# Sums of squares from squares split into a rounded high part and its rest, in a two-block transformer kernel on one core

## What is computed

```python
def rms_norm(x, g):
    y = xf * lax.rsqrt(jnp.mean(xf * xf, axis=-1, keepdims=True) + RMS_EPS)
    return (y * g.astype(jnp.float32)).astype(x.dtype)

def l2norm(x):
    return xf * lax.rsqrt(jnp.sum(xf * xf, axis=-1, keepdims=True) + EPS)

q = partial_rope(rms_norm(q, q_norm_g), positions)      # block 1; k_sel and k_win likewise
qa = l2norm(qa.reshape(b_, t_, GDN_HEADS, GDN_DK))      # block 2; ka likewise
```

## Time and profile before

| | |
|---|---|
| median of 3 runs | 1579.89 us (1577.96 to 1580.7) |
| the profiled execution | 1581.75 us |
| its span, first to last instruction | 1580.0 us |
| TensorE busy | 1545.2 us, 98% |
| VectorE, ScalarE, GpSimd busy | 898.0, 571.1, 207.5 us |
| mean granted TensorE clock | 0.994 |

### The profile page before, as it was taken

How to read it: one execution, slowest core, us unless ns; L and a number is a source line. 1 busy time by engine, 2 the same in 40 slices (tenths; PEclk the granted TensorE clock), 3 DMA queues, 4 the chain that set the end, 5 groups by cost and what they waited for, 6 DMA issues and landing times.

```text
span 1580.0 us, 21479 instructions
## 1 busy us (share of the span) xinstructions
PE 1545.2 (98%) x7712; PEld 1237.0 (78%) x7712; DVE 898.0 (57%) x1437; ACT 571.1 (36%) x874; POOL 207.5 (13%) x263
## 2 busy tenths in 40 slices
PE   9999999999999999999999999989999999999997
PEld 6876676788888888887787778766788888888885
DVE  6138666565666665334763642346466888887233
ACT  6134466544333332223225313236544322332221
POOL 2557212100000000000002351232100000000000
PEclk9999999999999999999999999999999999999999
DMA  6523112333222233222232251252332232233221
GB/s 213 215 74 101 60 48 81 122 132 107 85 101 95 91 106 117 92 93 72 93 107 94 100 137 41 85 197 77 140 135 95 95 103 93 93 102 120 95 92 71
DMA packets 58244, 164.72 MB, mean 104 GB/s; under 512 B 11952, under 2 KB 12344, under 8 KB 58048
## 3 DMA queue, kind: packets, MB, share of 16 engines
q1 hardware_dynamic: 52928, 158.07, 28.7%
q10 hardware_dynamic: 5248, 5.74, 1.1%
HBM read 148.83 MB, written 14.96 MB: 104 GB/s over the span
## 4 chain that ended last, share of the span: by engine, by line
PE 90%; DVE 5%; ACT 2%; DMA 2%; issue 1%; ACTq 0%; SPq 0%; DVEq 0%; POOL 0%
PE banks L1687 27%; PE banks L1689 26%; PE banks L1688 26%; PE banks L1786 2%; PE banks L1797 2%; PE banks L1826 2%; PE banks L2067 1%; DMA w_raw<-in_w_in 0%; PE banks L2103 0%; PE banks L2082 0%; PE banks L2094 0%; PE banks L2024 0%; DMA w_raw<-in_w_mix 0%; PE banks L1993 0%; DVE state L1635 0%
## 5 line engine op out<-in xcount | busy, mean ns | idle before, releaser
L1687 PE MATMUL banks<-h_hi,w_hi 128*128 128x512 f32 x1312 | 530.5, 404 | 7.2 <-POOL w_lo L562 2.7
L1688 PE MATMUL banks<-h_lo,w_hi 128*128 128x512 f32 x1312 | 512.3, 390 | 0.0
L1689 PE MATMUL banks<-h_hi,w_lo 128*128 128x512 f32 x1312 | 512.2, 390 | 0.0
L790 ACT ACTIVATE w_hi<-w_raw 128x1024 fp32r<-128x1024 f32 (+1 forms) x226 | 249.3, 1103 | 468.3 <-PE banks L1689 418.6
L1687 PEld LDWEIGHTS banks<-h_hi,w_hi 128*128 128x128 f32 x1312 | 247.0, 188 | 93.0 <-issue 28.8
L1689 PEld LDWEIGHTS banks<-h_hi,w_lo 128*128 128x128 f32 x1312 | 246.7, 188 | 52.9
L1688 PEld LDWEIGHTS banks<-h_lo,w_hi 128*128 128x128 f32 x1312 | 247.1, 188 | 52.4 <-issue 5.0
L554 DVE TENSOR_TENSOR w_lo<-w_raw,w_hi 128x1024 fp32r<-128x1024 f32 (+1 forms) x168 | 217.9, 1297 | 83.0 <-ACT w_hi L790 82.8
L562 POOL TENSOR_TENSOR w_lo<-w_raw,w_hi 128x256 fp32r<-128x256 f32 x232 | 178.6, 802 | 374.0 <-ACT w_hi L790 374.0
L1687 PE MATMUL banks<-act_hi,w_hi 128*128 128x512 f32 x352 | 136.9, 389 | 0.0
L1688 PE MATMUL banks<-act_lo,w_hi 128*128 128x512 f32 x352 | 136.9, 389 | 0.0
(11 more groups left out here) (291 smaller groups left out, 1741.4 us busy)
## 6 DMA issues: line engine op xcount, KB each, us to landing
w_raw<-in_w_up SPq DMA_DIRECT2D x88, 512.0 KB, 3.4
w_raw<-in_w_fill SPq DMA_DIRECT2D x44, 512.0 KB, 3.5
w_raw<-in_w_down SPq DMA_DIRECT2D x32, 704.0 KB, 4.0
late_scratch<-stage SPq DMA_DIRECT2D x44, 256.0 KB, 2.0
w_raw<-in_w_mix SPq DMA_DIRECT2D x16, 512.0 KB, 4.3
sg<-late_scratch SPq DMA_DIRECT2D x16, 512.0 KB, 3.8
w_raw<-in_w_out SPq DMA_DIRECT2D x16, 512.0 KB, 3.5
w_raw<-in_w_in SPq DMA_DIRECT2D x13, 512.0 KB, 3.5
```

Source lines behind the costliest of these rows:

```text
L790: act.activation(w_hi[:, c.slot, 0:kt * P], w_raw[:, c.slot, 0:kt * P], ACT.Copy)\
L1687: pe.matmul(dst, w_h, hi[:, kr, :], start=first and n == 0, stop=False)
L1688: pe.matmul(dst, w_h, lo[:, kr, :], start=False, stop=False)
L1689: mm = pe.matmul(dst, w_l, hi[:, kr, :], start=False, stop=last and n == len(ks) - 1)
```

## The change

In both places the plain float32 product of a sum is replaced by two products in fp32r. ScalarE squares each tile twice, once to float32 and once to fp32r, which rounds; VectorE subtracts the two (`rest_of_square`); TensorE multiplies both parts by an fp32r copy of `halves` or `ones` that ScalarE makes once per block, and adds them in the same bank. The rests of tiles 0 and 1 are made ahead of VectorE's loop, that of tile n+2 right behind the scaling of tile n. One semaphore is saved by counting the reduction of L1375 on `blk_done`. The core of the diff:

```diff
-            def inverse_roots(tiles, sq, rt, s_sq, s_ms, s_ln, s_inv, s_used, scale, serve=None, behind={}):
+            def inverse_roots(tiles, sums, sq, hi, rt, s_sq, s_ms, s_ln, s_inv, s_used, scale, serve=None, behind={}):
 
                 def square(n):
                     wait(act, s_ms, n - 1)
                     act.activation(sq[:, n % 2, :], tiles[n], ACT.Square).then_inc(s_sq, 1)
+                    act.activation(hi[:, n % 2, :], tiles[n], ACT.Square).then_inc(s_sq, 1)
+                act.activation(sums[0][:, :], sums[1], ACT.Copy).then_inc(s_sq, 1)
                 square(0)
                 square(1)
...
+            def rest_of_square(sq, hi, lo, s_sq, s_low, n):
+                dve.wait_ge(s_sq, 2 * n + 3)
+                sub(lo[:, n % 2, :], sq[:, n % 2, :], hi[:, n % 2, :]).then_inc(s_low, 1)
+
             serve = late("fill1", 0, FILL1, FILLED1, stage1)
+            for n in range(2):
+                rest_of_square(nr_sq, nr_hi, nr_lo, n_sq, n_low, n)
             for n, (t, gain) in enumerate(tiles):
                 dve.wait_ge(n_inv, n + 1)
                 dve.scalar_tensor_tensor(p1[:, t, :], p1[:, t, :], gain, nr_r[:, n % 2, :], ALU.mult, ALU.mult)\
                     .then_inc(n_gain, 1)
+                if n + 2 < 6:
+                    rest_of_square(nr_sq, nr_hi, nr_lo, n_sq, n_low, n + 2)
                 if n:
                     rotate(n - 1)
                 serve("norm", n)
...
             for n in range(6):
-                pe.wait_ge(n_sq, n + 1)
+                pe.wait_ge(n_low, n + 1)
                 wait(pe, n_ln, n - 1)
-                pe.matmul(bank(BS + n % 2), halves, nr_sq[:, n % 2, :], start=True, stop=True).then_inc(n_ms, 1)
+                pe.matmul(bank(BS + n % 2), halves_r[:, :], nr_hi[:, n % 2, :], start=True, stop=False)
+                pe.matmul(bank(BS + n % 2), halves_r[:, :], nr_lo[:, n % 2, :], start=False, stop=True).then_inc(n_ms, 1)
```

More of the change, by code:

```diff
@@ L272, in two_blocks @@
         nr_sq = area("nr_sq", [P, 2, T], F32, 62)
+        nr_hi = area("nr_hi", [P, 2, T], F32R, 78)
+        nr_lo = area("nr_lo", [P, 2, T], F32R, 62)
+        halves_r = area("halves_r", [P, P], F32R, 93.5)
         nr_r = area("nr_r", [P, 2, T], F32, 66)
@@ L315, in two_blocks @@
         l2_sq = area("l2_sq", [P, 2, T], F32, 78)
+        l2_hi = area("l2_hi", [P, 2, T], F32R, 86)
+        l2_lo = area("l2_lo", [P, 2, T], F32R, 78)
+        ones_r = area("ones_r", [P, P], F32R, 98.25)
         l2_r = area("l2_r", [P, 2, T], F32, 82)
@@ L427, in two_blocks @@
         l_sq, l_ms, l_ln, l_inv, l_out = (sem("l_" + x) for x in ("sq", "ms", "ln", "inv", "out"))
+        n_low, l_low = sem("n_low"), sem("l_low")
         turned = [sem(f"turned{b}") for b in (1, 2)]
@@ L431, in two_blocks @@
         pad_zero, blk_zero = sem("pad_zero"), sem("blk_zero")
-        gather_made = sem("gather_made")
         pooled = sem("pooled")
@@ L973, in _ @@
             serve = late("fill1", FILL1, FILLED1)
-            inverse_roots([p1[:, t, :] for t in (4, 5, 6, 7, KS, KW)], nr_sq, nr_r, n_sq, n_ms, n_ln, n_inv,
+            inverse_roots([p1[:, t, :] for t in (4, 5, 6, 7, KS, KW)], (halves_r, halves), nr_sq, nr_hi, nr_r, n_sq, n_ms, n_ln, n_inv,
                           n_gain, 1.0 / DH, serve, {1: hidden_parts})
@@ L1037, in _ @@
             serve = late("fill2", FILL2, FILLED2)
-            inverse_roots([p2a[:, t, :] for t in range(8)], l2_sq, l2_r, l_sq, l_ms, l_ln, l_inv, l_out, 1.0, serve)
+            inverse_roots([p2a[:, t, :] for t in range(8)], (ones_r, ones), l2_sq, l2_hi, l2_r, l_sq, l_ms, l_ln, l_inv,
+                          l_out, 1.0, serve)
             g = slice(32, 32 + GH)
@@ L1374, in _ @@
                 by_sixteen(p1[:, KC + c, :], c, 0, 32).then_inc(blk_done, 1)
-            dve.tensor_reduce(gather[:, :], ident.rearrange("p (q n) -> p n q", q=4), AXX, ALU.add).then_inc(gather_made, 1)
+            dve.tensor_reduce(gather[:, :], ident.rearrange("p (q n) -> p n q", q=4), AXX, ALU.add).then_inc(blk_done, 1)
             tiles = [(t, param("q_gain")) for t in (4, 5, 6, 7)] + [(KS, param("k_gain", 1, 1)),
@@ L1500, in _ @@
             serve = late("fill2", 1, FILL2, FILLED2, stage2)
+            for n in range(2):
+                rest_of_square(l2_sq, l2_hi, l2_lo, l_sq, l_low, n)
             for n in range(8):
@@ L1504, in _ @@
                                          l2_r[:, n % 2, :], ALU.mult, ALU.mult).then_inc(l_out, 1)
+                if n + 2 < 8:
+                    rest_of_square(l2_sq, l2_hi, l2_lo, l_sq, l_low, n + 2)
                 serve("norm", n)
@@ L1888, in add_parts @@
                 pe.wait_ge(c_act, 1)
-                pe.wait_ge(gather_made, 1)
+                pe.wait_ge(blk_done, 6)
                 for c in range(2):
@@ L1990, in _ @@
             for n in range(8):
-                pe.wait_ge(l_sq, n + 1)
+                pe.wait_ge(l_low, n + 1)
                 wait(pe, l_ln, n - 1)
-                pe.matmul(bank(BS + n % 2), ones, l2_sq[:, n % 2, :], start=True, stop=True).then_inc(l_ms, 1)
+                pe.matmul(bank(BS + n % 2), ones_r[:, :], l2_hi[:, n % 2, :], start=True, stop=False)
+                pe.matmul(bank(BS + n % 2), ones_r[:, :], l2_lo[:, n % 2, :], start=False, stop=True).then_inc(l_ms, 1)
                 fill("norm", n)
```

## The result

The changed kernel takes 1584.29 us (median of 13 runs, 1580.21 to 1587.09) against 1579.89 (13 runs, 1577.27 to 1581.39): ratio 1.0026, 95% interval 1.0018 to 1.0034. It is 4.4 us slower where the forecast said 1.6 slower. The time lies inside the range (1578.3 to 1584.9), the likeliest case does not hold: "within 0.2%" had 0.60, and what came is the slower side, which had 0.29.

What follows compares the result with a forecast made beforehand. TensorE was taken to bound the kernel; block 1's +2.25 and block 2's -0.75 us gave +1.5, applied to the median as 1579.89 + 1.6, rounded up: 1581.5 us, range 1578.3 to 1584.9.

Steps and rivals of the forecast that it cites:

- the likeliest case: Whole kernel: time within 0.2% (3.2 us) of the kernel before, chance 0.60.
- the slower side: Whole kernel: slower than before by more than 0.2% (3.2 us), chance 0.29.
- The saving: TensorE's 14 sums in both blocks: two passes save 0.40 us per sum, 5.6 us in all.
- Waits ahead of the first sums: TensorE waits for VectorE's rest of tile 0: 1.85 us in block 1, 0.5 us in block 2.
- Waits for the copy: Behind odd tiles TensorE waits for VectorE's late chunk copy: 1.4 us twice in block 1, 0.65 three times in block 2.
- its second rival: VectorE held longer beside GpSimd in odd tiles: +3.6, or +4.4 with block 1's rotation; 1583.5 to 1584.3 us, chance 0.12.
- The sum of the local terms: Waits less savings: block 1 +2.25 us, block 2 -0.75, together +1.5 us.
- what was to be hidden: ScalarE's second squares (0.55 us each) and GpSimd's weight rests, in both blocks, would not delay TensorE.
- the rival of a fall: Clock falls to 1.2 GHz behind a new wait, costing 1.8 us; total +3.4, 1583.3 us, chance 0.2.

Runs made afterwards that it cites:

- no_rest: Changed kernel with both passes multiplying the rounded square and VectorE's rests left out; 1575.35 us, ratio 0.9976 to the kernel before.
- the two short-pooled kernels: Last group's pooling on 64 of 512 columns, in the kernel before (1577.68 us) and in early_and_behind (1572.52 us).
- early_and_behind: Changed kernel with tile 0's rest made earlier and tile n+2's rest behind rotation and copy; 1577.00 us, ratio 0.9990 to the kernel before.

## Why the prediction missed the likeliest case

**The saving.** Right. 0.40 per sum was forecast; 0.40 is measured (0.45 against 0.85), and no_rest shows it by itself.

**Waits ahead of the first sums.** Right in place, a little short. Forecast 1.85 and 0.5; a wait's bracket counts from the end of the last record, which lies 0.39 - 0.23 = 0.16 behind the point where the queue was free, so the brackets 2.00 and 0.41 are 2.16 and 0.57. The rest came when forecast (98.28 against 98.2); TensorE was there 0.2 earlier, at 96.1.

**Waits for the copy.** Right in place and number, under-sized in block 1. Forecast 1.4 twice, measured 1.68 and 1.62 plus 0.16, so 1.8; forecast 0.65 three times, measured 0.52 to 0.59 plus 0.16, so 0.7. ScalarE's second square ended 4.02 behind the sum's start (forecast 4.05), and the rest took 1.06 (forecast 1.13). What was too small is the rotation, 2.85 us from 111.97 to 114.82 where 2.44 had been read off: its first product now ran beside GpSimd's work as well, 1.21 against 0.68. The prediction had that in its second rival, at 0.45 a tile. And some 0.15 between the copy's end and TensorE's next start were left out. The Trainium skill (SBUF — State Buffer, SBUF: two separate sides) has such operations wait for the whole of a GpSimd one; the trace agrees that they are lengthened, by 0.38 and 0.53 here, which is less than the whole of a GpSimd operation (3.73 / 4 = 0.93) and near the half that an encounter at a random moment would give.

**The sum of the local terms.** With measured sizes: block 1 2.16 + 3.6 - 2.4 = +3.4, block 2 0.57 + 2.1 - 3.2 = -0.5, together +2.9 instead of +1.5. The places confirm it: +3.0 at the transposes, -0.3 in block 2. It is the low end of the 3 to 3.6 that runs at equal clock show. Of what was to be hidden, the rests of block 2's even tiles were forecast at 0.68 us and took 0.69, 1.18 and 1.10; VectorE stood idle behind them, and nothing came of it.

**The clock.** This is the step that failed: the forecast took "granted clock 1.00 behind the waits" as the likeliest, and the rival of a fall had 0.2. In the first profile it did hold at the new waits, in the second a fall behind the 2.00 us wait cost 1.5. The rival's price was near (1.8 forecast). Its chance did not follow from its own condition: it was to decide "if the wait is nearer to 1.7 than to 1.3", and the prediction's own value for that wait was 1.7 (it is 2.00), so by its own reading the fall was the likelier case, at 0.2. And it was treated as happening or not, where it happens in part of the executions. On average the clock added 1 to 2 us, about 0.9 of it by the estimate above at the first sum; the fall behind the pooled products is in most profiles, whatever the kernel, and nothing here shows that it has a part in the 4.4. Local sum and clock give 4 to 5, the measured 4.4. The waits for the copy, 0.4 too small in block 1, are the other term that was short. Whether the slower side would have been reached without the clock is not settled: 2.9 by itself is within 0.2% (3.2 us), the 3.6 of runs at equal clock is not.

**What stays open.** Why the clock falls behind the same wait in one execution and not in the next. What else scatters the spans of runs at the same mean clock. And how much of block 1's saving could be had if VectorE's stretch from 120 to 150 and GpSimd's rests were both shorter.

## What to carry to other kernels

A product saved on the bounding engine is worth its time only if its new input is ready: here 0.40 us per sum was bought with a second operation on each of two helpers, and the first tile, with nothing to do meanwhile, cost five tiles' savings. Put the helper's new operation behind whatever another consumer waits for, and early for the first tile; then follow the saving to the next place where the helper is busy without a break, for that is where it ends. Lay one kernel's profile against more than one of the other before calling a step at one place the change's: here 1.4 us at 152 was a fall of the clock that seven of eight profiles have. Price a new wait near 2 us on TensorE as itself plus a share of a fall of the clock, and compare kernels by many executions, since one profile of each (0.1 us apart here) can hide the whole effect.

## What the runs showed of the hardware

The granted clock is not a function of the wait. Behind 2.41 us it was lower in one profile of before and 1.00 in another; behind 2.00 lower in three of five. Waits of 0.4 to 1.7 in the norms showed no fall behind them in the changed kernel's first profile. Behind the wait of 2.4 us ahead of the pooled products it fell in seven of eight profiles, behind one of 2.20 at the same place in the two short-pooled kernels in neither. A fall costs about the same each time: the four pooled products took 3.44 to 3.65 us in six profiles and 3.18 in one, instead of 1.96, and the first sum's fall cost 1.5. In `early_and_behind`, behind two waits of 2 us in a row, the clock was 0.51 over 6 us. Over the table of spans, 0.001 of mean clock goes with some 1.4 us in the kernel before (1580.0 at 0.994, 1575.8 at 0.997) and 1.5 in the changed one (1584.6 at 0.993, 1578.4 at 0.997), with a scatter of up to 5 us between runs at the same clock.

VectorE's operations are longer beside GpSimd's, by very different amounts: a subtraction or rotation product of two SBUF operands by 0.38 and 0.53 us beside rests of weights, a scaling by 3.5 us (4.29 against 0.83) beside a fill with zeros of 3.52.
